# Two row passes and two product passes: sums of h on VectorE, and other places for the gate chain, the state steps and attention's loads

## What is computed

```
mod = silu(c) @ w_ada + b_ada; shift, scale, gate = split(mod, 3)
h = rmsnorm(x, norm_w) * (1 + scale) + shift
proj = h @ w_in + b_in                # 2048 x (9*512 + 16)
na_q, na_k, na_v, na_z, ml_q, ml_k, ml_v, ml_o, ml_z, i_f, f_f, i_b, f_b = split(proj)
na_out = neighbourhood_attention(na_q, na_k, na_v, rpb) * silu(na_z)
mq, mk = split(silu(centred_short_conv([ml_q, ml_k])))
h_fwd = mlstm_chunkwise(mq, mk, ml_v, i_f, f_f)       # a state carried over chunks
h_bwd = flip(mlstm_chunkwise(flip(mq), flip(mk), flip(ml_v), flip(i_b), flip(f_b)))
hm = layernorm((h_fwd + h_bwd) * sigmoid(ml_o)) * ml_norm_w * silu(ml_z)
x = x + gate * ([na_out, hm] @ w_out); out = rmsnorm(x, final_norm_w)
```

## Time and profile before

| | us |
|---|---|
| median of 3 runs (1877.6 to 1879.27) | 1878.28 |
| the profiled execution | 1877.82 |
| its span | 1876.0 |
| PE busy in it | 1824.4 (97%) |
| DVE busy | 1175.3 (63%) |
| ACT busy | 755.6 (40%) |
| POOL busy | 737.8 (39%) |
| mean granted clock | 0.988 |

### The profile page before, as it was taken

One profiled execution on the slowest core, in us unless ns is written; L12 is line 12 of the kernel. 1 busy time (PEld: TensorE's weight loads), 2 busy tenths in 40 slices (PEclk: granted clock), 3 DMA queues, 4 the chain that ended last, 5 costly groups with the idle time before them and its releaser, 6 DMA issues.

```text
span 1876.0 us, 27028 instructions
## 1 busy us (share of the span) xinstructions
PE 1824.4 (97%) x9747; PEld 1496.2 (80%) x9747; DVE 1175.3 (63%) x2348; ACT 755.6 (40%) x1551; POOL 737.8 (39%) x1038
## 2 busy tenths in 40 slices
PE   9999999999999999999999789999998999999998
PEld 8888878888887788888877568888876777788886
DVE  6556565773667443777753647667754777776665
ACT  7321111232544322544442224444334667655553
POOL 2112222232652242444432414555424777544442
PEclk9999999999999999999999889999999999999999
DMA  6223242357896823334475313688677776767663
GB/s 195 98 79 117 63 130 76 109 171 219 297 320 225 285 82 97 117 94 144 128 228 193 86 51 109 182 274 262 222 243 214 236 228 221 269 212 241 231 230 113
DMA packets 261521, 332.48 MB, mean 177 GB/s; under 512 B 43270, under 2 KB 175270, under 8 KB 261356
## 3 DMA queue, kind: packets, MB, share of 16 engines
q1 hardware_dynamic: 230876, 244.75, 42.3%
q0 software_dynamic: 23600, 77.61, 11.5%
q10 hardware_dynamic: 6912, 8.39, 1.3%
HBM read 223.61 MB, written 107.54 MB: 177 GB/s over the span
## 4 chain that ended last, share of the span: by engine, by line
PE 84%; DVE 6%; DMA 4%; POOL 3%; issue 2%; ACT 1%; SPq 1%; POOLq 0%; DVEq 0%; ACTq 0%
PE banks L158 23%; PE banks L160 22%; PE banks L159 22%; PE banks L2591 3%; PE banks L2573 2%; PE banks L2554 2%; PE banks L3203 2%; PE banks L3205 1%; PE banks L2896 1%; DVE op L1590 1%; DVE ring L1590 1%; PE banks L3173 1%; PE banks L2574 1%; DMA wgr<-in_w_in 1%; PE banks L247 1%
## 5 line engine op out<-in xcount | busy, mean ns | idle before, releaser
L158 PE MATMUL banks<-op,ring 128*128 128x512 f32 x672 | 266.9, 397 | 2.3 <-DVE ca L1942 1.5
L160 PE MATMUL banks<-op,ring 128*128 128x512 f32 x672 | 264.4, 393 | 0.0
L159 PE MATMUL banks<-op,ring 128*128 128x512 f32 x672 | 264.1, 393 | 0.0
L158 PE MATMUL banks<-hT,wu 128*128 128x512 f32 (+1 forms) x528 | 204.8, 388 | 1.1 <-DVE wu L525 0.6
L160 PE MATMUL banks<-hT,wu 128*128 128x512 f32 (+1 forms) x528 | 202.6, 384 | 0.0
L159 PE MATMUL banks<-hT,wu 128*128 128x512 f32 (+1 forms) x528 | 202.4, 383 | 0.0
L158 PEld LDWEIGHTS banks<-op,ring 128*128 128x128 f32 x672 | 127.0, 189 | 29.7 <-DVE ca L1942 1.9
L160 PEld LDWEIGHTS banks<-op,ring 128*128 128x128 f32 x672 | 126.8, 189 | 28.2
L159 PEld LDWEIGHTS banks<-op,ring 128*128 128x128 f32 x672 | 127.1, 189 | 27.0
L1590 DVE TENSOR_TENSOR ring<-praw,ring 128x512 fp32r<-128x512 f32 x160 | 140.9, 907 | 7.1 <-ACT ring L1585 6.5
L1973 DVE SCALAR_TENSOR_TENSOR ca<-cu,cw,ca 128x512 f32<-128x512 f32 (+2 forms) x128 | 115.5, 902 | 35.8 <-ACT ca L1829 34.6
(11 more groups left out here) (314 smaller groups left out, 4247.3 us busy)
## 6 DMA issues: line engine op xcount, KB each, us to landing
opraw<-hT SPq DMA_DIRECT2D x17, 1024.0 KB, 9.6
wa<-in_w_ada SPq DMA_DIRECT2D x48, 256.0 KB
praw<-in_w_in SPq DMA_DIRECT2D x12, 1024.0 KB, 8.9
praw<-in_w_in SPq DMA_DIRECT2D x24, 512.0 KB, 4.1
praw<-in_w_in SPq DMA_DIRECT2D x48, 256.0 KB, 3.8
yT<-sg POOLq DMA_DIRECT2D x32, 256.0 KB, 3.1
oraw<-yT SPq DMA_DIRECT2D x32, 256.0 KB, 5.7
xr<-in_x SPq DMA_DIRECT2D x16, 512.0 KB, 5.2
```

Source lines behind the costliest of these rows:

```text
L158: e.matmul(ps, lh, rh, start=first, stop=False, skip_group_check=more)
L159: e.matmul(ps, lh, rl, start=False, stop=False, skip_group_check=more)
L160: return e.matmul(ps, ll, rh, start=False, stop=last, skip_group_check=more)
```

## The change

- The T sums leave plan_sums and POOL and go to DVE (sum_h): both halves at items 11 and 12 of the first block, and at the first two nv tiles of the second block, right behind the tile's evacuation. All four instructions of a half now wait for each other in turn, on a semaphore of their own. The splits of T come x within t, one item later in the second block.
- The gate chain's ticks are laid out again over the same ten items, so that no item holds more than one product on PE.
- In the second pass the state ticks stand 13/7 items apart instead of 2: 27 of the 33 lie in the pass and 6 in the last tiles, before it was 25 and 8.
- Attention: four nq loads go two items ahead of the last tiles, the four nk loads of the same columns to the first of them, the tables to the second (before the sixth), and POOL's mid goes to the sixth (before the seventh).

```diff
--- before.py
+++ after.py
@@ -1278,6 +1278,7 @@
         self.copied, self.joined = k.sem("copied"), k.sem("joined")
         self.tapped, self.evac, self.conv_step, self.conv_u = k.follow(mixer.g_hi, 4), k.sem("evac"), k.sem("conv_step"), k.sem("conv_u")
         self.row_step, self.gsum, self.low, self.sums = k.sem("row_step"), k.sem("g_sum"), k.sem("nk_low"), k.follow(mixer.g_lo, 4)
+        self.h_sums = k.follow(mixer.wt_turned, 16)
         self.lane, self.v_st = k.dsems("lane", 4, "pool"), k.dsems("v_st", 2)
 
         work = [("mv", m) for m in range(8)] + [("gates", 0), ("gates", 1)] + [("nv", m) for m in range(8)] + [("mo", m) for m in range(8)]
@@ -1350,7 +1351,7 @@
         pre, post = {}, {}
         early = {13: rows(0, 0, 4), 14: half(0), 15: half(1)}
         put = lambda d, n, js: d.setdefault(n, []).extend(js)
-        sums = [("t", ps, x, t) for ps in range(2) for x in range(2) for t in ("T1", "T3", "T2", "T4")]
+        sums = [("t", ps, x, t) for ps in range(2) for t in ("T1", "T2", "T3", "T4") for x in range(2)]
         put(pre, 0, rows(0, 4, 8))
         put(post, 1, half(2))
         put(post, 2, half(3))
@@ -1382,7 +1383,7 @@
         put(post, r + 2, [("gates", 1)])
         put(pre, self.item[("mv", NT - 1)], rows(4, 0, 8))
         for i in range(8):
-            put(post, r + 10 + i, [sums[8 + i]])
+            put(post, r + 11 + i * 7 // 8, [sums[8 + i]])
         put(pre, self.mo0, rows(5, 6, 8))
         put(post, self.mo0, half(8))
         self.early, self.pre, self.post = early, pre, post
@@ -1395,7 +1396,7 @@
 
     def plan_sums(self):
 
-        at = {11: [("t", 0, 0)], 13: [("t", 0, 1)], self.second + 9: [("t", 1, 0)], self.second + 11: [("t", 1, 1)]}
+        at = {}
         for ps in range(2):
             c0 = self.c0[ps]
             for q in range(NQ):
@@ -1407,8 +1408,10 @@
         self.sums_at, self.sum_of, n = at, {}, 0
         for x in sorted(at):
             for s in at[x]:
-                n += 4 if s[0] == "t" else 1
+                n += 1
                 self.sum_of[s] = n
+        r = self.second
+        self.t_sums_at = {11: [(0, 0)], 12: [(0, 1)], r + 10: [(1, 0)], r + 11: [(1, 1)]}
 
     def plan_outputs(self):
 
@@ -1471,9 +1474,9 @@
     def plan_ticks(self):
 
         r, c0 = self.second + 8, self.c0[1]
-        gates = ((0, 1, 2), (3, 4), (5,), (6, 7), (8, 9), (10,), (11,), (12, 13, 14), (15,), (16, 17))
+        gates = ((0, 1, 2), (3, 4, 5), (6,), (7, 8), (9, 10), (11,), (12,), (13, 14, 15), (16,), (17,))
         self.ticks = {r + i: list(ts) for i, ts in enumerate(gates)}
-        at = [c0 + 34 + 2 * i for i in range(25)] + [self.mo0 + m for m in range(8)]
+        at = [c0 + 34 + 13 * i // 7 for i in range(27)] + [self.mo0 + m for m in range(6)]
         self.ticks_sp = {r - 1: [0]}
         for i, n in enumerate(at):
             self.ticks[n] = [18 + i]
@@ -1561,7 +1564,7 @@
         elif j[0] == "h":
             w.wait_ge(*self.h_in[j[1] % 2].ge(j[1] // 2 + 1))
         elif j[0] == "t":
-            w.wait_ge(*self.sums.ge(self.sum_of[("t", j[1], j[2])]))
+            w.wait_ge(*self.h_sums.ge(8 * j[1] + 4 * j[2] + 4))
         else:
             if j[0] == "row":
                 w.wait_ge(*self.raw_in[self.raw_set(j)].ge(self.raw_loads(j)))
@@ -1770,7 +1773,7 @@
                 self.load_h(e, w, 8)
             for t in self.ticks_sp.get(n, ()):
                 states.sp(e, w, t)
-            if n >= mo0:
+            if n >= mo0 - 2:
                 att.early_sp(e, w, n - mo0)
             if x[0] == "nv":
                 m, i = x[1], self.st_of[n]
@@ -2026,6 +2029,8 @@
                 self.free(w, b, n)
                 e.tensor_tensor(self.buf[b][:], self.pg(n), self.br[:, int(name == "nv"), :], ALU.add).then_inc(*self.row_step.inc())
             out.tail_dve(e, w, n)
+            for ps, y in self.t_sums_at.get(n, ()):
+                self.sum_h(e, w, ps, y)
             if row:
                 for j in self.post.get(n, ()):
                     self.split_low(e, w, j)
@@ -2034,19 +2039,20 @@
             for t in self.ticks.get(n, ()):
                 states.dve(e, w, t)
 
+    def sum_h(self, e, w, ps, x):
+
+        w.wait_ge(*self.t_in.ge(4 * ps + 4))
+        a, b, d, c = (self.opraw[self.tslot[ps][t]][:, 2 * x:2 * x + 2] for t in ("T1", "T3", "T2", "T4"))
+        e.tensor_tensor(a, b, a, ALU.subtract).then_inc(*self.h_sums.inc())
+        w.wait_ge(*self.h_sums.last())
+        e.tensor_tensor(b, d, b, ALU.subtract).then_inc(*self.h_sums.inc())
+        w.wait_ge(*self.h_sums.last())
+        e.tensor_tensor(d, d, a, ALU.subtract).then_inc(*self.h_sums.inc())
+        w.wait_ge(*self.h_sums.last())
+        e.tensor_tensor(c, c, d, ALU.subtract).then_inc(*self.h_sums.inc())
+
     def sum(self, e, w, s):
 
-        if s[0] == "t":
-            _, ps, x = s
-            w.wait_ge(*self.t_in.ge(4 * ps + 4))
-            a, b, d, c = (self.opraw[self.tslot[ps][t]][:, 2 * x:2 * x + 2] for t in ("T1", "T3", "T2", "T4"))
-            e.tensor_tensor(a, b, a, ALU.subtract).then_inc(*self.sums.inc())
-            e.tensor_tensor(b, d, b, ALU.subtract).then_inc(*self.sums.inc())
-            w.wait_ge(*self.sums.last())
-            e.tensor_tensor(d, d, a, ALU.subtract).then_inc(*self.sums.inc())
-            w.wait_ge(*self.sums.last())
-            e.tensor_tensor(c, c, d, ALU.subtract).then_inc(*self.sums.inc())
-            return
         _, ps, q, x = s
         r = lambda y: self.a_raw(ps, q, y)
         w.wait_ge(*self.raw_in[(q + 1) % 2].ge(self.raw_loads(("a", ps, q))))
@@ -2349,14 +2355,15 @@
     def early_sp(self, e, w, i):
 
         proj = self.proj
-        if i < 4:
-            w.wait_ge(*proj.full.ge(proj.mo0))
-            for name in ("nq", "nk"):
-                proj.stored_all(w, name)
+        if i in (-2, 0, 2, 3):
+            w.wait_ge(*proj.full.ge(proj.mo0 + min(i, 0) - 1 + (i >= 0)))
+            if i == -2:
+                for name in ("nq", "nk"):
+                    proj.stored_all(w, name)
             for j in self.jobs:
-                if j[0] == "q" and j[2] == i:
+                if j[0] == "q" and ((j[2] < 2 and j[1] // 2 == (i == 0)) if i <= 0 else j[2] == i):
                     self.load(e, w, 0, j)
-        if i == 5:
+        if i == 1:
             for j in self.jobs:
                 if j[0] == "t":
                     self.load(e, w, 0, j)
@@ -2509,7 +2516,7 @@
                     e.memset(mid[32 * ri:32 * ri + 32, :, :, c0:c1], NEG).then_inc(*self.blocked.inc())
 
     def early_pool(self, e, w, i):
-        if i == 6:
+        if i == 5:
             for part in range(4):
                 self.block(e, w, 0, part)
 
```

## The result

| | before | after |
|---|---|---|
| median | 1878.42 us (1877.6 to 1879.27, 4 runs) | 1848.55 us (1847.05 to 1851.35, 4 runs) |
| ratio, 95% interval | | 0.9843 (0.9826 to 0.986) |
| span of the profiled execution | 1876.0 | 1846.9 |
| mean granted clock | 0.988 | 0.998 |

The forecast was 1848, in a range of 1839 to 1860.

What follows compares the result with a forecast made beforehand. PE, busy 1824.4 of 1876.0 us, was taken as the bound. From 1877.82, gates -28, attention -5 and states +3 gave 1847.8 for the profiled execution, so a median of 1848, range 1839 to 1860.

Steps and rivals of the forecast that it cites:

- The walk: Following the gate chain through the new order beside the second block's eight nv tiles, pricing each wait: 28 us less.
- The stretch: Second block's eight nv tiles beside the gate chain: 51.8 us, against 78.2 + 1.7 before.
- wait at R: Behind the second nv tile, DVE's sums and splits delay a small product's operand: 3.5 us stays, replacing 3.1.
- L: Gate chain result PE waited 6.0 us for; ready before the first nv tile ends, so that wait goes.
- uT and mpB: Later gate chain results, waited for 2.0 and 6.5 us; ready well before PE needs them, so both waits go.
- The semaphore between DVE instructions: Four dependent T sums on DVE: if semaphores cost nothing, 4.5 us instead of 4.95, and R's wait 3.1 instead of 3.5.
- The diagnosis: Beside the nv tiles, POOL's T sums stretch DVE's two-input instructions, so gate chain results come late and PE waits.
- ring: PE's waits for a split, 6.0 us together; about 4.2 goes once the splits run without sums beside them.
- Denser states: State steps closer together in the second pass make PE wait for POOL's weighed v: 3 us more, bounds 0 to 12.
- half a microsecond for each other: Second pass: wait allowed for each closely spaced pair of state steps after the first, which was taken in full at 1.6.
- Rival A: POOL late in the second pass, full waits and low clock at all four pairs: states cost 10 to 16, chance 0.13.
- Attention's start: Last tiles: waits for scores, pg and e and low clock go, 0.8 lost for sv: 5 us less, bounds 0 to 8.

Runs made afterwards that it cites:

- e1: Kernel before with only the T sums moved to DVE, old steps, states and attention kept; ratio 0.9965, 6.6 us less.
- e2: Kernel before with only the gate chain's new step order, T sums still on POOL; ratio 0.9917, 15.6 us less.
- e4: Kernel before with only the second pass's state steps set at 13/7 items; ratio 1.0012, 2.3 us more.
- e11: Changed kernel with the second pass's state steps two items apart again; ratio to before 0.9825, 32.9 us less.
- e3: Kernel before with only attention's loads and POOL's mid moved as in the change; ratio 0.9963, 7.0 us less.
- e8: Changed kernel with DVE taking the gate chain's steps ahead of sums and T splits in the second block's nv tiles; ratio to before 0.9816.
- e5: Changed kernel plus ten unused POOL instructions, one memset and nine in-place subtractions on its own tile; ratio to before 0.9911, 16.7 us less.
- e6: Changed kernel plus twenty unused POOL memsets of 128 x 1024, which only write; ratio to before 0.984, 30.1 us less.

## Why the prediction was right, and where it was not

- **The mechanism and the number.** The walk that gave the number held in its waits; the account of why the old waits were there did not, and that the total still came out to 1 us is partly luck, as the bullets show.
- **The stretch.** Forecast 51.8, measured 51.60. The one wait at R was forecast at 3.5 and is 3.4; PE's busy 48.17 is 44.2 plus 4.0 for small products and the low clock behind that wait (2.4 + 1.7 forecast). The waits came as the walk had them: dependent sums at 1.25 to 1.26 each (forecast 4.95 for four, 4.91 seen), L in time, uT and mpB without a wait. Only the eight splits missed their sign, 5.60 instead of 4.9, and L had room for it: DVE had it at 1035.2, and PE asked for it at 1036.33.
- **The semaphore between DVE instructions.** The Trainium skill, *VectorE: DVE Perf Modes*, "The DRAIN you can't avoid", finds for eight tensor_copy that a semaphore after each costs nothing extra; carried over to these four subtractions that was 1.13 each, 4.5. The trace differs by 0.12 an instruction: 1.25 for a dependent sum, 1.13 for an independent one of the same size. The wait at R, 3.1 by that reading and 3.5 by the forecast, was 3.4.
- **The diagnosis failed.** "So the chain's DVE results come late and PE, in order, stands at the small products" puts all five waits down to POOL's T sums. e1 shows that only ring (4.2) and L (6.0) were theirs; mpB, R and uT, 11.6 us, stay to 0.1 us without any T sum on POOL, and e2 shows that the new order alone takes them away. The total came out right since the walk used the new order at every step. It would have been wrong for either edit alone, and the expectations of e1 and e2, written with the result in hand, were: rows that name DVE as the releaser do not say whether DVE was slow or was doing something else first. mpB had both: six splits ahead of its copy, and those six stretched to 8.2 us beside POOL's sums of weights, which the prediction did not look at.
- **Denser states.** Forecast 3 more (0 to 12); the trace has 1.7 at the first pair (forecast 1.6), 2.4 at the second and 0.6 for a state at another. The term "half a microsecond for each other" pair was too small for the second, where the weighing stands behind two sums of 1.29 and 1.60: 4.7 of waits. In time the part costs 2 to 3 (e4, e11), since a state wait of 1.0 at attention's scores goes. Rival A did not come: no low clock followed these waits, the clock of the pass is 1.00.
- **Attention's start.** The term was sized too small: forecast 5 less (0 to 8), measured 7.0 alone (e3) and some 9.2 - 1.8 = 7.4 in the whole. pg fell to 0.8 and e went, as said; the 0.8 set against it for a later sv did not show (swv waits 1.4 in the last tiles, 1.8 before).
- **The sum.** -28 - 5 + 3 = -30 forecast; 28.5 for the gates (26.6 and the 1.9 behind), 7.4 for attention, about 4.7 for the states and 1.4 of drift in the unchanged start make 29.8, and 29.1 was seen. Attention was better by 2.4 and the states worse by 1.7, in opposite directions, which is luck for the sum.

## What to carry to other kernels

A wait that a profile puts down to an engine is a question, not an answer: read what stands ahead of the releasing instruction in its queue, and whether those instructions take their usual time; the first is mended by the order, the second by what runs beside them, and one wait can have both, as mpB's had. Two edits that meet in one chain should be judged together, here 27.2 us against 6.6 + 15.6. And when work moves onto the engine that feeds the bottleneck, put the small results that someone waits for ahead of it: that edit (e8) gained about 5 us on top of the change.

## What the runs showed of the hardware

- A DVE instruction with two SBUF inputs can be held for longer than one POOL instruction: u, 0.29 alone, took 5.05 across two sums of 2.4. In the same way the two M scans took 2.54 and 2.39, about one sum each, instead of 0.87 for both.
- The hold is not in proportion to size: 128 x 1 took 1.19 instead of 0.16 in e5.
- POOL's memset of 128 x 1024 takes 1.0 us and stretches nothing on DVE in e6 (splits 5.60, u 0.29); its two-input instruction of that size takes 2.0 to 2.3 and stretches eight splits from 5.6 to 12.
- After a wait of 3.4 PE's next three full matmuls start 0.24 to 0.34 apart, as the first ones behind a small product do without any wait, and the slow ones (0.62 to 0.63 long) begin 0.8 us after the first:

```profile
1052.27 0.50 PE L158 MATMUL banks<-ring,op 128*128 128x512 f32 x1
1052.61 0.40 PE L159 MATMUL banks<-ring,op 128*128 128x512 f32 x1
1052.85 0.43 PE L160 MATMUL banks<-ring,op 128*128 128x512 f32 x1
1053.09 0.62 PE L158 MATMUL banks<-ring,op 128*128 128x512 f32 x1
```
